# Block 0 of the first FFN without its down products: norms one tile ahead, down products carried into block 1

## The reference, cut to what matters

```python
h = modulate(rms_norm(x, g_ff1), sh1, sc1)        # x * rsqrt(mean(x*x)+eps) * g * (1+sc1) + sh1
a, u = split(h @ w_ff1_in)                        # 1024 -> 2 x 2816
x = x + 0.5 * g1 * ((silu(a) * u) @ w_ff1_out)    # 2816 -> 1024
```

## Time and profile before

| | us |
|---|---|
| median of three runs (1687.8 to 1692.62) | 1688.66 |
| profiled execution | 1701.97 |
| its span, core 3 (the slowest; cores 1680.7 to 1700.4) | 1700.4 |
| TensorE busy / VectorE / ScalarE / GpSimd | 1536.0 / 956.5 / 494.2 / 158.2 |

### The profile page before, as it was taken

One profiled execution on the slowest core, in us unless ns is written; L12 is line 12 of the kernel. 1 busy time (PEld: TensorE's weight loads), 2 busy tenths in 40 slices (PEclk: granted clock), 3 DMA queues, 4 the chain that ended last, 5 costly groups with the idle time before them and its releaser, 6 DMA issues.

```text
span 1700.4 us, 25281 instructions; the slowest of 8 cores (1680.7 to 1700.4 us)
## 1 busy us (share of the span) xinstructions
PE 1536.0 (90%) x8548; PEld 695.4 (41%) x8548; DVE 956.5 (56%) x1646; ACT 494.2 (29%) x739; POOL 158.2 (9%) x235
## 2 busy tenths in 40 slices
PE   1689999999999995698889888999999999999998
PEld 1234444444444442243434444444334444444443
DVE  2256556555566554464546665345366666666666
ACT  2651110111111125745636566235421111111110
POOL 2131000000000012300000000021210000000000
PEclk9799999999999997787889899999999999999999
DMA  9906442345432332457225355584322222222005
GB/s 183 243 1 91 75 67 37 48 74 76 75 48 43 59 87 99 101 116 142 37 56 120 99 113 113 138 186 75 50 38 38 37 38 38 38 38 38 13 1 198
DMA packets 35788, 134.68 MB, mean 79 GB/s; under 512 B 5072, under 2 KB 5200, under 8 KB 33616
## 3 DMA queue, kind: packets, MB, share of 16 engines
q0 software_dynamic: 22560, 79.88, 30.3%
q1 hardware_dynamic: 13104, 53.18, 9.3%
HBM read 191.95 MB, written 20.97 MB: 125 GB/s over the span
## 4 chain that ended last, share of the span: by engine, by line
PE 79%; DVE 6%; issue 5%; ACT 4%; DMA 4%; POOL 1%; DVEq 0%; ACTq 0%; SPq 0%; POOLq 0%
PE ps L413 76%; ACT arena L422 3%; DVE arena L430 3%; PE ps L410 3%; DMA arena<-wts 3%; DVE arena L426 2%; POOL arena L603 1%; DMA arena<-xin 1%; DVE arena L436 1%; ACT L422 1%; DVEq L183 0%; DVE arena L445 0%; DVE arena L442 0%; ACTq L183 0%; POOL arena L323 0%
## 5 line engine op out<-in xcount | busy, mean ns | idle before, releaser
L413 PE MATMUL ps<-arena 128*128 128x512 bf16 (+3 forms) x7108 | 1476.7, 363 | 132.9 <-DVE arena L430 53.5
L413 PEld LDWEIGHTS ps<-arena 128*128 128x128 bf16 x7108 | 646.7, 100 | 919.6 <-issue 336.8
L430 DVE SCALAR_TENSOR_TENSOR arena<-ps,arena 128x512 f32<-128x512 f32 (+2 forms) x860 | 562.5, 714 | 89.6 <-ACT arena L422 47.1
L422 ACT ACTIVATE arena<-ps 128x512 f32<-128x512 f32 (+4 forms) x418 | 266.1, 652 | 1045.8 <-PE ps L413 526.7
L426 DVE TENSOR_TENSOR arena<-arena,ps 128x512 bf16<-128x512 f32 (+1 forms) x198 | 130.2, 658 | 411.7 <-PE ps L413 382.4
L426 DVE TENSOR_TENSOR arena<-arena 128x512 f32<-128x512 f32 (+10 forms) x196 | 141.6, 738 | 114.9 <-ACT arena L422 89.3
L323 POOL DMA_DIRECT2D arena<-wts x150 | 79.9, 536 | 1255.5 <-PE ps L413 1025.0
L422 ACT ACTIVATE arena<-arena 128x512 bf16<-128x512 f32 (+6 forms) x230 | 165.6, 748 | 86.9 <-DVE arena L426 25.0
L410 PE MATMUL ps<-arena 128*128 128x65 bf16 (+3 forms) x1440 | 80.6, 214 | 25.5 <-DVE arena L436 16.0
L603 POOL TENSOR_TENSOR arena<-arena 128x512 bf16<-128x512 f32 (+3 forms) x77 | 75.9, 1010 | 186.4 <-ACT arena L422 99.3
L410 PEld LDWEIGHTS ps<-arena 64*128 64x128 bf16 (+1 forms) x1440 | 53.5, 98 | 79.0 <-issue 69.8
(11 more groups left out here) (12 smaller groups left out, 6.1 us busy)
## 6 DMA issues: line engine op xcount, KB each, us to landing
arena<-wts POOLq DMA_DIRECT2D x150, 512.0 KB, 8.8
arena<-xin SPq DMA_DIRECT2D x8, 1024.0 KB, 13.6
xspill<-arena SPq DMA_DIRECT2D x4, 2048.0 KB, 7.0
arena<-xspill SPq DMA_DIRECT2D x4, 2048.0 KB, 14.7
yoT<-arena SPq DMA_DIRECT2D x32, 256.0 KB, 2.3
arena<-ebias SPq DMA_DIRECT2D x12, 640.0 KB, 5.1
arena<-ebias SPq DMA_DIRECT2D x8, 768.0 KB, 5.4
nkT<-arena SPq DMA_DIRECT2D x8, 256.0 KB, 2.9
```

The costliest lines, as they stand in the source:

```text
L413: return P.emit("pe", lambda e: e.matmul(out, lhsT=lhsT, rhs=rhs, start=start, stop=stop), reads=reads, writes=writes, inc=inc)
L422: return P.emit("act", lambda e: e.activation(out=out, in_=in_, func=func, **kw), reads=reads, writes=writes)
L430: return P.emit("dve", lambda e: e.scalar_tensor_tensor(out=out, in0=in0, scalar=scalar, in1=in1, op0=op0, op1=op1), reads=reads, writes=w ...
```

## The change

Block 0 has no down products any more: after the G and U products of all five tiles come ada 8 to 11, and block 1 computes both blocks' down products, block 0's ("owed") for tile t in step t, its own a step behind as before. The hb products of block 0 are kept for all five tiles in a buffer of their own, `HB5`, and block 0's down weights stay in their slot until the end of block 1. In block 0 the norm of tile t+1 (part b) and the squares of tile t+2 (part a) are issued ahead of both halves of tile t (for tile 0, ahead of the second half). All these norms use the eight temporaries, all multiplies are VectorE's, and modulations alternate between ScalarE and VectorE. Squares go to ScalarE, GpSimd and VectorE for tile 1, and to GpSimd and ScalarE (chunks 3 and 7) for tiles 2 to 4. Tiles 1 to 4 of x are loaded behind weight units 7, 9, 11, 12 in place of 6, 10, 13, 15.

```diff
+        HB5 = mem(oG + 16384, 10240, BF16, "p (t j n) -> p t j n", t=5, j=2)
+        P.claim(oG + 16384, 10240, [("hb5", t, j) for t in range(5) for j in range(2)])
...
-            nt = 8 if mid is not None else 2
-            TB_ = TMP8 if mid is not None else TB
+            big = wide or mid is not None
+            nt = 8 if big else 2
+            TB_ = TMP8 if big else TB
...
+        def hbuf(hs):
+            return (HB, "hb", hs) if hs < 2 else (HB5, "hb5", hs - 2)
...
-                for ti, u in ((1, 6), (2, 10), (3, 13), (4, 15)):
+                for ti, u in ((1, 7), (2, 9), (3, 11), (4, 12)):
                     lazy_load(ti, after=wtok[u])
                 norm_tile(nidx, tiles[0], part="b", mo="av", stat=stat0, mid=lambda: first_mod(acc))
+                norm_tile(nidx, tiles[1], part="a", sq="apv")
...
-                if not first:
-                    ud, Dn, rd = wacq(("ffd", which, bi))
+                if first:
+                    for t in range(ntt):
+                        if t + 1 < ntt:
+                            if t == 0:
+                                ff_GU(G, U, rg, ru, nj, tiles[t], 2 + t, jjs=[0])
+                            norm_tile(nidx, tiles[t + 1], part="b", mo="av", wide=True)
+                        if t + 2 < ntt:
+                            norm_tile(nidx, tiles[t + 2], part="a", sq="pppapppa")
+                        ff_GU(G, U, rg, ru, nj, tiles[t], 2 + t, jjs=[1] if t == 0 else [0, 1])
+                    wrel(ug)
+                    wrel(uu)
+                    blk0_hook()
+                    owed = wacq(("ffd", which, bi))
+                    after_block(bi)
+                    continue
+                ud, Dn, rd = wacq(("ffd", which, bi))
...
-                        if first and step + 1 < ntt:
-                            norm_tile(nidx, tiles[step + 1], sq="a" if step == 0 else "pppppppa",
-                                      sc="vvvp" if step else "v")
-                        if first and step == 1:
-                            blk0_hook()
-                            ud, Dn, rd = wacq(("ffd", which, bi))
...
+                        if owed is not None and step < ntt:
+                            ff_DN(owed[1], owed[2], nj, tiles[step], 2 + step, ig, ms=[m])
                         if step >= 1:
                             ff_DN(Dn, rd, nj, tiles[step - 1], (step - 1) % 2, ig, ms=[m],
...
                 wrel(ud)
+                if owed is not None:
+                    wrel(owed[0])
+                    owed = None
```

More of the change, by code:

```diff
@@ L618, in norm_stat, with norm_gen @@
             return b
-        def norm_gen(nidx, tile, part="ab", sq="pa", sc="v", mo="a", mid=None, stat=None, gap=0):
+        def norm_gen(nidx, tile, part="ab", sq="pa", sc="v", mo="a", mid=None, stat=None, gap=0, wide=False):
             ib = nidx * 3
@@ L649, in norm_gen @@
             yield 1
-            nt = 8 if mid is not None else 2
-            TB_ = TMP8 if mid is not None else TB
-            tag = "tb8" if mid is not None else "tb"
+            big = wide or mid is not None
+            nt = 8 if big else 2
+            TB_ = TMP8 if big else TB
+            tag = "tb8" if big else "tb"
             def scaled(c):
@@ L690, in build_program @@
         silc = [0]
+        def hbuf(hs):
+            return (HB, "hb", hs) if hs < 2 else (HB5, "hb5", hs - 2)
         def ff_GU(G, U, rg, ru, nj, tile, hs, jjs=None):
+            hb, hkey, hi = hbuf(hs)
             t0, n, cond = tile
@@ L705, in ff_GU @@
                 actv(SIL[:, ss, 0:n], bank_ap(ba)[:, 0:n], AF.Silu, [banks[ba]], [P.R("sil", ss)])
-                vtt(HB[:, hs, jj, 0:n], SIL[:, ss, 0:n], bank_ap(bu)[:, 0:n], ALU.mult,
-                    [P.R("sil", ss), banks[bu]], [P.R("hb", hs, jj)])
+                vtt(hb[:, hi, jj, 0:n], SIL[:, ss, 0:n], bank_ap(bu)[:, 0:n], ALU.mult,
+                    [P.R("sil", ss), banks[bu]], [P.R(hkey, hi, jj)])
         def ff_DN(Dn, rd, nj, tile, hs, ig, ms=range(8), chunk_done=None):
             t0, n, cond = tile
+            hb, hkey, hi = hbuf(hs)
             for m in ms:
@@ L713, in ff_DN @@
                 for jj in range(nj):
-                    mm(bank_ap(by)[:, 0:n], Dn[:, jj, m * 128:(m + 1) * 128], HB[:, hs, jj, 0:n],
-                       jj == 0, jj == nj - 1, [rd, P.R("hb", hs, jj)], [banks[by]], inc=(jj == nj - 1))
+                    mm(bank_ap(by)[:, 0:n], Dn[:, jj, m * 128:(m + 1) * 128], hb[:, hi, jj, 0:n],
+                       jj == 0, jj == nj - 1, [rd, P.R(hkey, hi, jj)], [banks[by]], inc=(jj == nj - 1))
                 vstt(xview(m, t0, n), bank_ap(by)[:, 0:n], DER[:, ig, m, cond:cond + 1], xview(m, t0, n),
```

## The result

| us | before | after |
|---|---|---|
| median of three runs | 1688.66 (1687.8 to 1692.62) | 1716.29 (1716.27 to 1717.35) |
| ratio after / before, 95% interval | | 1.0159 (1.0134 to 1.0185) |
| profiled execution | 1701.97 | 1716.29 |
| its span | 1700.4 | 1714.4 |

What follows compares the result with a forecast made beforehand. Block 0's norm chain was taken to delay block 1's closed-up TensorE products: start 121.3 plus 68.4 us ends at 189.7 against 187.3, so 1688.7 + 2.4 = 1691.1 us; own range 1688 to 1694, all cases 1681 to 1697.

Steps and rivals of the forecast that it cites:

- Nothing in it is peculiar to this core: Profiled execution: claimed nothing specific to its core, so the 2.4 us loss was added to the median 1688.7 us.
- The U wait: Block 1's start: U weights reuse block 0's G slot, are issued late and need 6.2 us; a 1.7 us stall.
- other losses: Rival: half clock at block 1's start, or block 1's bursts at their upper bound; chance 0.08.
- The norm chain: Block 0: norms set the pace, 13.3 us a tile against TensorE's 8.6; block 1's G done at 121.3 us.
- A closed-up run on one engine keeps the other out to its end: Shared SBUF port in block 0: VectorE and GpSimd exclude each other for longer than one instruction; 3.38 us cited.
- VectorE first: Rival in block 0: VectorE keeps the port until its norm ends, GpSimd follows; 1.8 us faster, 1686.9 us, chance 0.25.
- GpSimd first: Rival in block 0: GpSimd keeps the port through later squares, delaying tile 2's norm; 6.0 us slower, 1694.7 us, chance 0.20.
- No collision: Rival in block 0: squares always finish before the norm starts; 6.3 us faster, 1682.4 us, chance 0.15.
- bursts: Block 1: eight DN outputs in a row per half step wait for VectorE's evictions; 4.5 us, bounds 0 to 8.

Runs made afterwards that it cites:

- e9: The changed kernel again, unaltered, beside the kernel before: 1702.6 us without a slow pair, 12.4 us slower than before, ratio 1.0071.
- e4: Changed kernel with block 1's U weights in their own buffer, loaded early: 1695.8 us without a slow pair, 7.2 us slower than before.
- e10: Changed kernel with squares of tiles 2 to 4 alternating between ScalarE and VectorE, none on GpSimd: 1698.5 us, 8.3 us slower than before.
- e5: Changed kernel with six squares a tile left out (tiles 2 to 4) and block 1's U weights loaded early: 1687.2 us, ratio 0.9989 to before.
- e6: Changed kernel with four owed down outputs per half step put between its G and U products: 1692.3 us, 4.4 us slower than before.
- e8: The kernel before, unchanged, run once more for a second profile: 1687.01 us, no slow pair.

## Why the prediction was wrong

The sign was right, the size and the range were not: 27.6 us for 2.4. Two steps failed: a pair of cores at 0.81 had no term, and the wait for U was put at 1.7 us. Without a pair the changed kernel takes 1702.6 us, also outside 1681 to 1697, so the first step alone doesn't explain the miss.

- **The pair at 0.81 (15 us, the largest; no term in the sum).** "Nothing in it is peculiar to this core" was false: the spans show core 3 (and 2) of the kernel before 13 us and more above the others, at a clock of 0.79 in one stage. The sentence didn't move the sum, since the 2.4 us were added to the median, 1688.7, and not to the profiled time. What it did was to leave out a risk: a third level of the clock was in the profile read for the forecast, with a price of some 14 us, and it had no chance and no width in the range. In its place the three runs all had a pair at that level, and e9, without one, takes 13.7 us less; what sets it off stays open. The Trainium skill (TensorE: Matmul & The Clock Gate, Seeing it yourself) does know a current limiter that takes the clock to 13/16, 0.81, for the whole die. Level and price are in our rows; the whole die is not: core 2 stood at 1.00 beside core 1 at 0.81 on the same die.
- **The U wait (3 us in the median core, 5 in the slowest).** Place and cause were right, the size was not: 1.7 us was put in, 1.8 to 6.7 came (e9 against e4). The 6.2 us from issue to landing of the earlier trace rows were one load's on one core; here 5.1 us (core 0) to 8.0 us (core 3) passed. And the lower clock behind a wait (0.64 on core 3, 0.57 on core 0 of e9) stood under "other losses" with 0.08, though the earlier trace rows show it at 0.50 in a stretch where TensorE was busy 4.66 of 10 us.
- **The norm chain (2 us).** Right in form and nearly in size: Exp of tile 4 at 110.0 for 108.2, tile 1's products at 74.97 for "near 76". First G of block 1 done at 123.3 in the median of e9's cores, for 121.3.
- **How the port is shared.** "A closed-up run on one engine keeps the other out to its end" was wrong for these runs. Two multiplies take 2.1 to 2.97 us beside a run of squares, so each waits 0.4 to 0.8 us, less than one square, and three squares beside multiplies take 4.23 us for 3.03: the engines take turns. The Trainium skill (SBUF — State Buffer, Who interferes with whom) states a hold for one instruction, and the trace agrees; the forecast set that rule aside on one row. Why that one multiply, at 1138.79 us, waited out three squares stays open. For the sum it mattered little, since adding both engines' times is right either way: e10 measures 2.6 us for the contention, net of the squares it moved.
- **Rivals.** "VectorE first" and "GpSimd first" both fall with the alternation. "No collision" is e5 without the U wait: 3.3 us ahead of before at block 2 (6.3 forecast).
- **Block 1.** Half steps 7.62 for 7.44 us, bursts 4.6 us for 4.5, stopped by VectorE's evictions as worked out. The prediction treated them as given, though e6 removes them by an order that costs nothing.
- **After block 1 (about 2 us).** The ada products that follow ran on core 2 at 0.77, and block 2's start at 0.81, where core 2 of e8 has 1.00 (187 to 195 us); from the last products of block 1 to block 2's first Silu 5.7 us pass, in e8 4.1. No term stood for it. It is not the change's alone: core 3 of the first profile of before has 0.67 and 0.50 there and needs 5.9 us.

```profile
193.00:197.00 4.00, 2.96 (x54) 1.88 (x54) 1.62 (x6) 0.00 (x0) 2.12 (x4) 0.77 1.06 212
197.00:201.00 4.00, 4.00 (x17) 1.63 (x16) 0.41 (x1) 0.60 (x1) 0.00 (x0) 0.81 1.06 210
```

At block 2 the parts are 2.4 forecast, 2.0 chain, 3.0 U wait, 1.2 more in block 1 (69.6 us on e4's core 2, for 68.4) and 1.6 after it: 10.2, measured 9.4. At the slowest core 12.4 were measured: the cores differ by some 5 us in the U wait, and the metric takes the worst. The spans bear this out: the median core of e9's comparable runs is 8.3 us behind that of the kernel before (1695.0 against 1686.7).

The stated range is also narrower than its own cases with the bounds for block 1's bursts: 1682.4 - 4.5 = 1677.9 to 1694.7 + 3.5 = 1698.2. The measured time lies outside either.

## What to carry to other kernels

Hold a profiled core's span against its neighbours stage by stage: a stretch at a third clock level is a term of its own with a width in the range, and any run can meet it or miss it. Where work is moved to make a start earlier, look for the load whose slot is freed by that same start; its wait comes with a slow restart behind it, and the slowest core's wait counts. Here carried work did better between the G and U products of its host, where it covers such a wait, than in a burst behind them: that one edit was worth 8 us.

## What the runs showed of the hardware

- A pair of neighbouring cores at a granted clock of 0.81 for some 145 us (115 to 260 us), the others on the die at 1.00 in 145 to 185 us; in comparable runs it costs the kernel before 10 to 14 us and the others 5 to 22, in 10 of 23 runs of before on one chip and in none of 12 and of 13 on two others, where runs of 1713 us and more had one.
- Two 128x512 multiplies from SBUF on VectorE: 1.29 us alone, 2.11 to 2.97 us beside GpSimd squares; three squares 3.03 us, and 4.23 beside multiplies.
- A 1 MB weight load, the first of six issued within some 3 us to an idle queue, landed after 5.1 to 8.0 us, depending on the core. After a wait of 4.63 us TensorE ran at a clock of 0.64 in the stage behind it (128 to 132 us), after 1.87 us at 1.00, and in e9 after 3.50 us (core 2) at 1.00 too.
